# A two-block transformer kernel: where TensorE sums the first layer's shift and scale, and where VectorE accumulates the last two quarters of them

## The reference

```python
def diff_attention(q, k, v, lam, subln_g, lam_init):
    q = rotary(q, pos) * (DA_HEAD_DIM ** -0.5)
    k = rotary(k, pos)
    ...
    a = p[:, :, 0] - lam * p[:, :, 1]
    return einsum(a, v)
...
def second_block(x, c, w_ada, b_ada, ...):
    c_act = jax.nn.silu(c)
    for l in range(DEPTH_2):
        mod = c_act @ w_ada[l] + b_ada[l]
        shift, scale, gate = jnp.split(mod, 3, axis=-1)
        h = rmsnorm(x, g_pre[l]) * (1.0 + scale[:, None, :]) + shift[:, None, :]
```

## Time and profile before

| | |
|---|---|
| median of 3 runs | 1803.03 us (1802.95 to 1807.79) |
| the profiled execution's own time | 1807.16 us |
| its span in the profile | 1805.8 us |
| TensorE busy | 1629.6 us, 90% of the span |
| VectorE busy | 738.5 us, 41% |
| ScalarE busy | 483.4 us, 27% |
| GpSimd busy | 366.5 us, 20% |
| mean granted clock of TensorE | 0.945 of full speed |

### The profile page before, as it was taken

How to read it: one execution, slowest core, us unless ns; L and a number is a source line. 1 busy time by engine, 2 the same in 40 slices (tenths; PEclk the granted TensorE clock), 3 DMA queues, 4 the chain that set the end, 5 groups by cost and what they waited for, 6 DMA issues and landing times.

```text
span 1805.8 us, 15346 instructions
## 1 busy us (share of the span) xinstructions
PE 1629.6 (90%) x5808; PEld 795.6 (44%) x5808; DVE 738.5 (41%) x1525; ACT 483.4 (27%) x984; POOL 366.5 (20%) x348
## 2 busy tenths in 40 slices
PE   6699999999989799998788887999978999998898
PEld 3244446644454433333333333544455454445553
DVE  2916534345162411111010011469774143996622
ACT  2013243101031101000000002466365134645631
POOL 3610000100000111111110110148143012842500
PEclk9899999999999899889898889989999999999999
DMA  8321031456262699999999998401202120020101
GB/s 324 140 94 47 1 116 60 173 187 225 79 262 101 250 417 405 405 401 410 404 404 399 409 416 353 163 1 70 70 1 88 65 93 0 24 94 24 47 1 47
DMA packets 72977, 328.08 MB, mean 182 GB/s; under 512 B 10522, under 2 KB 13746, under 8 KB 60480
## 3 DMA queue, kind: packets, MB, share of 16 engines
q1 hardware_dynamic: 64976, 310.23, 44.2%
q0 software_dynamic: 6144, 10.52, 1.8%
q10 hardware_dynamic: 1776, 6.27, 0.9%
HBM read 320.60 MB, written 14.78 MB: 186 GB/s over the span
## 4 chain that ended last, share of the span: by engine, by line
PE 66%; DMA 20%; DVE 10%; ACT 2%; issue 1%; POOL 1%; DVEq 0%; ACTq 0%; POOLq 0%; SPq 0%
PE bank L187 62%; DMA arena<-in_w 15%; DMA arena<-h_rows,arena 3%; DVE arena L1264 2%; DVE arena L2551 1%; PE bank L2149 1%; DVE arena L2535 1%; PE bank L581 1%; POOL arena L1349 1%; DVE arena L2605 1%; DVE arena L2592 1%; DMA arena<-in_w_ada 0%; DMA arena<-in_params 0%; PE bank L666 0%; PE bank L906 0%
## 5 line engine op out<-in xcount | busy, mean ns | idle before, releaser
L187 PE MATMUL bank<-arena 128*128 128x512 f32 (+11 forms) x4944 | 1525.5, 551 | 100.4 <-DMA arena<-in_w 49.8
L187 PEld LDWEIGHTS bank<-arena 128*128 128x128 f32 (+5 forms) x4944 | 692.8, 178 | 865.6 <-issue 788.0
L2767 POOL TENSOR_TENSOR arena<-arena 128x512 f32<-128x512 f32 x180 | 205.2, 1140 | 223.7 <-ACT arena L2376 206.0
L1851 POOL TENSOR_TENSOR arena<-arena 128x1 f32<-128x1 f32 (+2 forms) x44 | 32.8, 746 | 598.3 <-DVE arena L1254 372.9
L1797 DVE TENSOR_TENSOR arena<-arena,bank 64x512 f32<-64x512 f32 x32 | 22.1, 691 | 314.0 <-ACT arena L1220 314.0
L2376 ACT ACTIVATE arena<-arena 128x512 f32<-128x512 f32 x180 | 126.2, 717 | 21.5 <-POOL arena L2767 21.3
L990 ACT COPY arena<-bank 128x512 f32<-128x512 f32 (+3 forms) x115 | 61.2, 538 | 248.6 <-PE bank L187 147.2
L1220 ACT ACTIVATE arena<-bank 64x512 f32<-64x512 f32 x32 | 18.9, 592 | 369.3 <-PE bank L187 369.3
L1872 POOL DMA_INDIRECT y_rows<-arena x32 | 32.1, 1004 | 413.4 <-PE bank L906 247.6
L1264 DVE SCALAR_TENSOR_TENSOR arena<-arena 128x512 f32<-128x512 f32 x84 | 78.4, 934 | 3.0
L1790 DVE TENSOR_TENSOR arena<-bank,arena 128x512 f32<-128x512 f32 x32 | 22.1, 692 | 112.0 <-PE bank L906 111.9
(11 more groups left out here) (264 smaller groups left out, 897.7 us busy)
## 6 DMA issues: line engine op xcount, KB each, us to landing
arena<-in_w SPq DMA_DIRECT2D x96, 2048.0 KB, 40.2
arena<-in_w_in SPq DMA_DIRECT2D x15, 2048.0 KB, 8.0
arena<-in_w_ada SPq DMA_DIRECT2D x12, 2048.0 KB, 9.2
arena<-in_w_out SPq DMA_DIRECT2D x6, 2048.0 KB, 7.7
arena<-in_w_xk SPq DMA_DIRECT2D x2, 2048.0 KB, 9.6
arena<-in_w_xv SPq DMA_DIRECT2D x2, 2048.0 KB, 10.6
arena<-in_w_xq SPq DMA_DIRECT2D x2, 2048.0 KB, 10.0
arena<-in_w_xo SPq DMA_DIRECT2D x2, 2048.0 KB, 9.1
```

Of the source, the lines that this page charges most:

```text
L187: i = pe.e.matmul(o, l, r, start=first and j == 0, stop=last and j == len(pairs) - 1)
L2767: pool.e.tensor_tensor(yc, yc, k.prod[l][n % 4], ALU.add).then_inc(*k.pool.step("sum", l, f, j))
```

## The change

1. TensorE sums the shift behind product 6 and no longer behind product 4.
2. TensorE sums the scale at tick 1 of the attention, in banks 4 and 5, and no longer behind product 6. The copy of it by VectorE and the store by ScalarE move to ticks 1 and 2.
3. VectorE runs rotations 4 and 5 ahead of the copy of the shift and of accumulation 2, and accumulation 3 behind rotation 7 and the copy of v0.

```diff
@@ pe_mixer_in
-        if g == 4:
+        if g == 6:
             pe_mod(k, pe, 0, 0)
-        elif g == 6:
-            pe_mod(k, pe, 0, 1)
@@ pe_diff_attention
         if tick in AMONG:
             pe_among(k, pe, *AMONG[tick])
+        if tick == 1:
+            pe_mod(k, pe, 0, 1, AMONG_BANKS)
@@ act_mixer_in
-        if g in (5, 7):
-            act_mod(k, act, 0, g // 2 - 2)
+        if g == 7:
+            act_mod(k, act, 0, 0)
@@ act_diff_attention
         if tick - 1 in AMONG:
             act_among(k, act, *AMONG[tick - 1])
+        if tick == 2:
+            act_mod(k, act, 0, 1)
@@ dve_mixer_in
-        elif g == 3:
+        elif g == 5:
             dve_mod(k, dve, 0, 0)
             dve_mods(k, dve, 2)
-        elif g == 4:
-            dve_mods(k, dve, 3)
-        elif g == 5:
-            dve_mod(k, dve, 0, 1)
-    for t in (0, 2):
-        dve_copy(k, dve, k.VV[:, t, :], B.at("v", t), "v", t)
+    dve_copy(k, dve, k.VV[:, 0, :], B.at("v", 0), "v", 0)
+    dve_mods(k, dve, 3)
+    dve_copy(k, dve, k.VV[:, 2, :], B.at("v", 2), "v", 2)
@@ dve_diff_attention
+        if tick == 1:
+            dve_mod(k, dve, 0, 1)
         dve_gates(k, dve, tick)
```

## The result

| | us |
|---|---|
| changed kernel, median of 4 runs | 1790.13 (1790.03 to 1790.31) |
| kernel before, median of 4 runs beside it | 1805.41 (1802.95 to 1808.38) |
| ratio | 0.9904, 95% interval 0.9883 to 0.9924 |
| the profiled execution: time, span, mean granted clock | 1790.03, 1788.7, 0.945 |

The change is faster by 1.0%, 15.3 us between the medians; 15.6 were forecast. The time of 1787.4 was 2.7 too low, nearly all of it because the median of before lies 2.4 higher here: these four runs are the three I started from and one more, of 1808.38. Timed once more beside the experiments, the changed kernel gave 1790.06 and a ratio of 0.9907 (0.9885 to 0.9929), 16.2 us beside a kernel before of 1806.23 (11 runs).

A forecast was written before the change was run, and what follows sets the result against it. TensorE's standstills were taken to bound the kernel. Terms -19.4 + 0.5 + 0.2 + 2.3 + 1.7 - 0.9 = -15.6 us gave 1787.4 from the 1803.03 median (chance 0.82), about 1783 to 1791; with A, 1782.5 to 1794.

The forecast's parts named there:

- What bounds: Whole kernel: what counts is where TensorE stands still (busy 90% of the span), not how much VectorE does.
- step 1: First stage: without its two TensorE holes, the copy of v3 starts 19.4 us earlier, with 0.48 for the shift's sum.
- Steps 2 to 4: Ahead of the attention: shift ready with 2.6 us to spare, rotation 7 at 89.6, accumulation 3 at 96.2; no cost.
- Step 5: Attention: scale's sum +0.5 us, gate rows' wait for v3's bank +0.2, new hole ahead of mqk 0 +2.3.
- Step 6: Attention: lower clock behind the new hole ahead of mqk 0 costs +1.7 us, bounds 0 and 3.4.
- Step 7: Behind the cross attention: later bank users move up, removing a 0.87 us wait for VectorE's line 1576: -0.9 us.
- Step 8: All later stages: loads hang on TensorE's progress, not wall time, so the shift is carried whole to the end.
- A: Attention gives back more, by longer holes and low clock: gain shrinks to about 9.5 us, 1793.5; chance 0.11.
- B: Expert stage: if its weight stream started at its own time, the gain would end there: 1803 us; chance 0.04.
- C: Attention: accumulation 3 late holds TensorE at the scale's sum, ahead of all scores; ending at 130, 1806.4 us; chance 0.03.

The follow-up runs named there:

- experiment 1: Changed kernel with VectorE's accumulations 2 and 3 back in their old order, behind rotations 3 and 4: 1791.77 us, ratio 0.9906.
- experiments 2: Changed kernel with the shift's sum back behind product 4, all else as changed: 1805.33 us, ratio 0.9979.
- experiment 6: Changed kernel with accumulation 3 moved behind the lambda, the last thing VectorE does ahead of the attention: 1795.29 us, ratio 0.9938.
- experiment 5: Changed kernel and kernel before, unedited, profiled once more: 1790.06 and 1805.59 us (one execution); it also compares the two profiles of experiment 3's version.
- experiment 3: Changed kernel with the scale's sum at tick 0, ahead of the gate rows: 1788.08 us, ratio 0.9880; again 1786.49 us, ratio 0.9881.

## Why the prediction was right, point by point

- **What bounds, and step 1: right.** TensorE's holes set the time: with one back, 13.6 us are back; with VectorE's order undone, nothing changes. 19.4 were forecast for the first stage and 19.06 came. The term off is the price of the shift's sum: I had 0.48 by subtraction from a stretch with two clocks in it, and it is 0.74 there.
- **Steps 2 to 4: right.** The shift was ready behind product 6 (no hole in the block), rotation 7 at 90.8 for 89.6, accumulation 3 at 97.3 for 96.2. The late us is a net of several: swap 5 ended 0.6 later, and the add of rotation 5 and the first instruction of accumulation 2 took 1.64 and 1.15 beside a swap, where I had them at their prices alone (0.69 and 0.48). Against that, the seven instructions of accumulation 2 took 10.82, where I had 11.6. I had read the same 10.82 of the kernel before as seven instructions beside a swap; six of them were, at 1.64 each, and one took 0.75.
- **Step 5: right.** The hole ahead of mqk 0 is 2.34 for 2.3, that for v3's bank 0.25 for 0.2, both by the bank that the diff picks without naming it. The sum of the scale is 0.5 for 0.5: from the first matmul of the gate rows to that of mqk 0 it was 7.62 us before (123.05 to 130.66), and is 10.45 now, of which the hole is 2.34. That is less than the 0.74 of the same four matmuls in the first stage.
- **Step 6, the clock: the sign was a guess and the term was wrong here.** I charged 1.7 behind the new hole. Neither profile of the changed kernel has it, nor that of experiment 1; experiments 2 and 6 have the same hole and the low clock, at just that price: 9.66 for 7.96 us. And I charged nothing for the other short holes, where low clock of the profiled execution before fell away (most of the 4.7 us that the table gains between the scores of step 4 and the memory rows). Of this, 2.7 was lost again in the cross attention and 1.8 in the experts and behind. The Trainium skill (TensorE: Matmul & The Clock Gate, HAM oscillation) warns only of longer idle gaps. The row that I set against it shows a low clock behind 1.25 us, and others here show one behind 0.90; yet the 2.34 went without one in three profiles of five, and a hole of 2.88 in the kernel before did too. The measurements bear out neither a cost behind every such gap nor none.
- **Step 7: right.** 0.9 forecast, 1.0 measured between the same two places, in all eleven traces.
- **Step 8: right.** Every later stage starts earlier by 16 to 21, and the end by 17.1. "Carried whole" is too strong for a difference that arises late: of the 2.79 us in the cross attention of experiment 5, a wait for a DMA took 1.8.
- **The rivals.** A (more given back in the attention) did not come: the holes there are unchanged to 0.01 us, but for the one of 0.82 that fell away. B did not either. C's mechanism is real, as experiment 6 shows, but the margin was there.

Without the later clock the measured terms are 15.93 at the scores of step 4 and 1.0 behind the cross attention, 17.0 in all; the two spans differ by 17.1, so the low stretches elsewhere came out even in this pair, which is luck. Between the second profiles the spans differ by 15.5 (1804.3 and 1788.8), between the medians of the first comparison by 15.3 and of the second by 16.2. That 15.6 lies so near to these is in part luck: it was 1.7 too dear behind the new hole, and it took the profiled execution of before, in which the clock was low behind every hole of the attention, as if nothing of that could change.

## What to carry to other kernels

An engine that runs in order pays for its place, not for its work: two sums of 0.5 to 0.7 us cost 19 between them, since each stood where its input was late and held a queue of ready products. Moving it needs no faster engine, only the time at which its input ends. When such an instruction moves among buffers handed out in turn, look up who held each buffer before: here that brought one hole of 2.34 us and took one of 0.87, and putting the sum in front of its neighbour kept the gain of the move without that hole. And where a change is worth a few us, measure what single holes do in the trace; the runs of the kernel before spread from 1802.5 to 1814.9 here.

## What the runs showed of the hardware

- The same hole in the same program is followed by a low clock in one execution and not in another: behind 3.68 us in the cross attention the stretch to the next hole took 16.57 and 13.81 us.
- A low stretch costs half of its length on gapless products: with the 3.4 us at 0.50 in them, 20 records of 7.96 us take 9.66, or 1.70 more, in both profiles that have one there.
- Where TensorE is not what bounds, a lower clock is not paid. From 600 to 1130 us, most of it the expert stage, the DMA engines are fully busy, and the changed kernel's two profiles have a mean granted clock of 0.89 and 0.91. From the experts' first transposes to the first wait for ScalarE's line 2324 in the second block, the one with 0.89 takes 577.6 us (598.14 to 1175.69), the other 578.8 (598.11 to 1176.91).
- A low stretch can swallow a hole. In the changed kernel the clock was low from 239.6 to 243.0, and the hole of 0.82 us that the kernel before has ahead of 270.51 is missing from its timeline: TensorE was late enough not to wait. The two profiles of experiment 3's version agree: the one with a low stretch at 238.6 has no such hole, the one without has 0.81 us, ahead of 247.16.
